# Attention values by head pairs in channel layout, and a merge written out unit by unit

## What is computed

```python
o_a = rms_norm(gated_delta_rule(...)) * silu(dn_z)          # branch 0
o_b = block_sweep_attention(b_qf, b_kf, b_v, scale, None)   # branch 1
o_c = rms_norm(gla_chunked(...)) * silu(gla_g)              # branch 2
o_d = block_sweep_attention(fox_q, fox_k, fox_v, scale, forget_cum)   # branch 3

# block_sweep_attention, for each block of 128 queries and each of 4 heads
logits = (q[block] @ k[:end].T) * scale (+ forget terms), masked
p = softmax(logits)
out = p @ v[:end]

merged = 0
for i in range(4):
    gate = sigmoid(h @ w_gate[i] + b_gate[i])
    merged = merged + gate * (branches[i] @ w_branch_up[i])
x = x + rms_norm(merged @ w_out, norm_mix_post)
```

## Time and profile before

| | |
|---|---|
| runs | 3096.55, 3099.35, 3099.67 us; median 3099.35 |
| profiled execution | 3094.74 us, span 3093.0 us |
| TensorE busy | 2818.3 us (91%), 14648 instructions |
| VectorE, ScalarE busy | 1431.7 us (46%), 952.0 us (31%) |
| mean granted TensorE clock | 0.966 |

### The profile page before, as it was taken

How to read it: one execution, slowest core, us unless ns; L and a number is a source line. 1 busy time by engine, 2 the same in 40 slices (tenths; PEclk the granted TensorE clock), 3 DMA queues, 4 the chain that set the end, 5 groups by cost and what they waited for, 6 DMA issues and landing times. The chain is left out here.

```text
span 3093.0 us, 35149 instructions
## 1 busy us (share of the span) xinstructions
PE 2818.3 (91%) x14648; PEld 2196.2 (71%) x14648; DVE 1431.7 (46%) x1621; ACT 952.0 (31%) x1291; POOL 121.2 (4%) x185
## 2 busy tenths in 40 slices
PE   6999998889978898987999999999389989999988
PEld 5767776567756676775888888888177768877776
DVE  2164442533142234846433434233746779842943
ACT  3141122333122433433323323121236622223122
POOL 0001110000000200100000100000000000000000
PEclk9999999999999999998999999999699999999999
DMA  3120011101112104621333333111320121112331
GB/s 105 43 74 32 29 39 56 55 29 48 52 47 72 49 23 159 212 63 48 109 96 96 102 96 98 53 48 48 122 75 28 48 68 58 52 41 96 106 116 68
DMA packets 66095, 220.81 MB, mean 71 GB/s; under 512 B 7608, under 2 KB 12504, under 8 KB 64288
## 3 DMA queue, kind: packets, MB, share of 16 engines
q1 hardware_dynamic: 51552, 165.01, 16.2%
q0 software_dynamic: 14400, 53.75, 5.1%
HBM read 179.93 MB, written 38.80 MB: 71 GB/s over the span
## 5 line engine op out<-in xcount | busy, mean ns | idle before, releaser
L280 PE MATMUL psum<-mixer_in,weights_parts 128*128 128x512 f32 x2112 | 504.4, 399 | 19.2 <-PEq L184 16.4
L280 PEld LDWEIGHTS psum<-mixer_in,weights_parts 128*128 128x128 f32 x2112 | 398.5, 189 | 118.4 <-issue 17.8
L424 PE MATMUL psum<-hidden,weights_parts 128*128 128x512 f32 x1536 | 433.8, 424 | 41.7 <-ACT early_gate L448 22.1
L247 DVE TENSOR_TENSOR weights_parts<-weights_raw,weights_parts 128x1024 fp32r<-128x1024 f32 (+2 forms) x195 | 211.4, 1084 | 386.7 <-ACT weights_parts L231 386.5
L424 PEld LDWEIGHTS psum<-hidden,weights_parts 128*128 128x128 f32 x1536 | 286.0, 195 | 127.4 <-issue 33.3
L280 PE MATMUL psum<-mlp_in,weights_parts 128*128 128x512 f32 x1536 | 352.3, 391 | 1.5 <-PEq L2418 1.5
L280 PE MATMUL psum<-mlp_hidden,weights_parts 128*128 128x512 f32 x1536 | 352.2, 391 | 0.0
L280 PEld LDWEIGHTS psum<-mlp_in,weights_parts 128*128 128x128 f32 x1536 | 288.4, 188 | 65.3 <-issue 2.3
L280 PEld LDWEIGHTS psum<-mlp_hidden,weights_parts 128*128 128x128 f32 x1536 | 288.5, 188 | 63.1
L280 PE MATMUL psum<-hidden,weights_parts 128*128 128x512 f32 x1200 | 279.2, 395 | 11.4 <-PEq L812 6.6
L231 ACT CAST weights_parts<-weights_raw 128x1024 fp32r<-128x1024 f32 (+2 forms) x195 | 182.2, 935 | 337.9 <-PE psum L280 223.7
(11 more groups left out here) (450 smaller groups left out, 3212.8 us busy)
## 6 DMA issues: line engine op xcount, KB each, us to landing
weights_raw<-in_w_in SPq DMA_DIRECT2D x73, 512.0 KB, 3.6
weights_raw<-in_w_mlp SPq DMA_DIRECT2D x64, 512.0 KB, 3.6
mod_weights<-in_mod_w POOLq DMA_DIRECT2D x80, 256.0 KB, 3.8
weights_raw<-in_w_gate SPq DMA_DIRECT2D x32, 512.0 KB, 3.7
gate_scratch<-early_gate SPq DMA_DIRECT2D x64, 256.0 KB, 2.2
gate<-gate_scratch POOLq DMA_DIRECT2D x32, 512.0 KB, 4.2
weights_raw<-in_w_out SPq DMA_DIRECT2D x24, 512.0 KB, 3.6
x_tokens<-in_x SPq DMA_DIRECT2D x4, 1024.0 KB, 8.1
```

The costliest lines, as they stand in the source:

```text
L247: nc.vector.tensor_tensor(c.parts[:, s, 1, 0:w], c.raw[:, s, 0:w], c.parts[:, s, 0, 0:w].bitcast(F32), ALU.subtract).then_inc(c.low_ready, 1)
L280: mm = nc.tensor.matmul(c.psum[:, bank + h, 0:cols], c.parts[:, s, wp, at], moving(k, xp, h), start=(n < halves), stop=(n >= halves * (3 * ...
L424: mm = nc.tensor.matmul(c.psum[:, bank, :], c.parts[:, s, wp, at], self.hidden[:, k, xp, h * HALF:(h + 1) * HALF], start=(k == 0 and n == ...
```

## The change

- `attend` multiplies the values of two heads at once, every second turn: v is the weights, the transposed probabilities move, and the heads of a pair write partitions 0 to 63 and 64 to 127. The output has channels on the partitions and is written to the branch's tile in SBUF. The reciprocal sums are spread over the channels by small products with the identity. The transposed probabilities have four buffers in place of two. The gate half is copied before the exponential of a turn.
- Branches 1 and 3 have no turning block; all 64 portions lie in `attend`, and halves from 4 on use bank 7. No branch is stored in DRAM. The turning of branches 0 and 2 writes to SBUF.
- The merge is written out as 32 units in the order `MERGE`, with units of branch 0 ahead; the branches are split tile by tile at units 0 to 2; a gate is loaded as soon as it is stored and its buffer is free; a bank is free after the product.
- The residual x is loaded by POOL in `mix_out`. Some scratch tiles of `latent_inputs`, `forgetting_inputs` and `add_residual` lie in others.

```diff
             @block.sync
             def _(sp):
-                if meanwhile:
-                    meanwhile(sp)
-                early.sp(sp, half)
-                if out is None:
-                    sp.wait_ge(vecs.sem, vecs.value("out"))
-                    store(c, sp, out_dram, o[:])
                 early.sp(sp, whole)
-                if out is None:
-                    sp.wait_ge(c.scratch_stored, c.stored)
         for s in (act, vecs, pes):
             s.end()
...
+def latent_attention(nc, c, t, hidden, small, early, out):
 
     with ExitStack() as ctx:
-        o_tok = c.sb("mla_out_tokens", [P, BLK, 256], ctx=ctx)
         v_tok = c.sb("mla_value_tokens", [P, BLK, 256], ctx=ctx)
         q, k = (c.sb(n, [P, HEADS, S], ctx=ctx) for n in ("mla_q", "mla_k"))
         with ExitStack() as inner:
             latent = c.sb("mla_latent", [P, 3, S], ctx=inner)
             project(nc, c, t["w_in"], 10, 3, hidden, latent)
-            early.begin(6, hidden, lambda half: 7 if 4 <= half < 10 else 6 + half % 2,
+            early.begin(6, hidden, lambda half: 7 if half >= 4 else 6 + half % 2,
                         (t["w_in"], 13, KT))
             latent_inputs(nc, c, t, latent, small, q, k, v_tok, early)
-        attend(nc, c, t, 0, 96, q, k, v_tok, o_tok, early, 48)
-        tokens_to_channels(nc, c, o_tok, t["branch"][1], early, 16)
+        attend(nc, c, t, 0, 96, q, k, v_tok, out, early, 64)
         early.end()
 
...
-                pe_spec.append(f"values{n - 1}")
+            if n and n % 2 == 0:
+                pe_spec += [(f"values{n // 2 - 1}", 2)]
                 if n % 4 == 0:
-                    vec_spec += [f"inverse{n // 4 - 1}", f"out{n // 4 - 1}"]
+                    pe_spec.append((f"spread{n // 4 - 1}", 2))
+                    vec_spec += [f"{s}{n // 4 - 1}" for s in ("inverse", "kept", "out")]
...
                     nk = (n // 4 + 1) * P
+                    early.act(a, upto(n - 1))
                     a.wait_ge(vecs.sem, vecs.value(f"max{n}"))
                     if n >= 2:
                         a.wait_ge(pes.sem, pes.value(f"turned{n - 2}"))
                     nc.scalar.activation(
                         prob[:, n % 2, 0:nk], scores(n, slice(0, nk)), ACT.Exp,
                         bias=neg_max[:, n % 2:n % 2 + 1], accum_out=sums[:, n:n + 1]).then_inc(act.step(f"exp{n}"), 1)
-                    early.act(a, upto(n - 1))
                     a.wait_ge(pes.sem, pes.value(f"turned{n}"))
-                    if n >= 2:
-                        a.wait_ge(pes.sem, pes.value(f"values{n - 2}"))
+                    if n >= 4:
+                        a.wait_ge(pes.sem, pes.value(f"values{n // 2 - 2}"))
                     m = min(nk, HALF)
-                    nc.scalar.copy(turned[:, n % 2, 0:m], c.psum[:, 4, 0:m]).then_inc(
+                    nc.scalar.copy(turned[:, n % 4, 0:m], c.psum[:, 4, 0:m]).then_inc(
                         act.step(f"low{n}"), 1)
                 early.act(a, e + portions)
...
                     v.wait_ge(act.sem, act.value(f"exp{4 * b + 3}"))
                     nc.vector.reciprocal(sums[:, s], sums[:, s]).then_inc(
                         vecs.step(f"inverse{b}"), 1)
-                    v.wait_ge(pes.sem, pes.value(f"values{4 * b + 3}"))
-                    v.wait_ge(vecs.sem, vecs.value(f"inverse{b}"))
+                    v.wait_ge(pes.sem, pes.value(f"spread{b}"))
+                    nc.vector.tensor_copy(spread[:], c.psum[:, 6, 256:512]).then_inc(
+                        vecs.step(f"kept{b}"), 1)
+                    v.wait_ge(vecs.sem, vecs.value(f"kept{b}"))
                     nc.vector.tensor_tensor(
-                        heads(o_tok[:, b, :]), heads(c.psum[:, 6, 0:256]),
-                        bcast(sums[:, s], DH), ALU.mult).then_inc(vecs.step(f"out{b}"), 1)
+                        out[:, :, b * P:(b + 1) * P],
+                        c.psum[:, 6, 0:256].rearrange("p (t n) -> p t n", t=2),
+                        spread[:].rearrange("p (t n) -> p t n", t=2), ALU.mult).then_inc(
+                        vecs.step(f"out{b}"), 1)
 
                 for n in turns:
...
+                def values(pair):
+
+                    b, t = pair // 2, pair % 2
+                    for m in (2 * pair, 2 * pair + 1):
+                        p.wait_ge(act.sem, act.value(f"low{m}"))
+                        if b >= 4:
+                            p.wait_ge(vecs.sem, vecs.value(f"high{m}"))
+                    if b and t == 0:
+                        p.wait_ge(vecs.sem, vecs.value(f"out{b - 1}"))
+                    for x in range(b + 1):
+                        for h in range(2):
+                            n = 2 * t + h
+                            last = mm(c.psum[64 * h:64 * h + 64, 6, t * P:(t + 1) * P],
+                                      v_tok[:, x, 64 * n:64 * n + 64],
+                                      turned[:, n, x * P:(x + 1) * P], start=(x == 0),
+                                      stop=(x == b))
+                            if x == b:
+                                last.then_inc(pes.step(f"values{pair}"), 1)
+
+                def spread_sums(b):
+
+                    p.wait_ge(vecs.sem, vecs.value(f"inverse{b}"))
+                    for t in range(2):
+                        for h in range(2):
+                            n = 4 * b + 2 * t + h
+                            last = mm(c.psum[64 * h:64 * h + 64, 6, 256 + t * P:256 + (t + 1) * P],
+                                      sums[:, n:n + 1].broadcast_to([P, DH]), c.ident[:],
+                                      start=True, stop=True)
+                            if t:
+                                last.then_inc(pes.step(f"spread{b}"), 1)
 
...
-                    if n:
-                        m = n - 1
-                        b, h = m // 4, m % 4
-                        p.wait_ge(act.sem, act.value(f"low{m}"))
-                        if b >= 4:
-                            p.wait_ge(vecs.sem, vecs.value(f"high{m}"))
-                        if b and h == 0:
-                            p.wait_ge(vecs.sem, vecs.value(f"out{b - 1}"))
-                        for x in range(b + 1):
-                            last = mm(c.psum[:, 6, 64 * h:64 * h + 64],
-                                      turned[:, m % 2, x * P:(x + 1) * P],
-                                      v_tok[:, x, 64 * h:64 * h + 64], start=(x == 0),
-                                      stop=(x == b))
-                        last.then_inc(pes.step(f"values{m}"), 1)
+                    if n and n % 2 == 0:
+                        values(n // 2 - 1)
+                        if n % 4 == 0:
+                            spread_sums(n // 4 - 1)
...
+MERGE = [(j, 0) for j in range(4)] + [
+    unit for j in range(8) for unit in [(j, 1), (j, 2), (j, 3)] + [(j + 4, 0)] * (j < 4)]
+SPLIT_AT = {0: [0, 1], 1: [2], 2: [3]}
...
+            for u in range(len(MERGE)):
+                for h in range(NH):
+                    pool.wait_ge(early.stored[h], 16 * (u + 1))
+                if u >= 4:
+                    pool.wait_ge(c.dve_done, d0 + sum(per_unit[:u - 3]))
+                pool.dma_start(gate[:, u % 4, :], t["gate"][u]).then_inc(loaded[u % 4], 16)
+
+        def sigmoid(a, u, j):
+            for x in SPLIT_AT.get(u, []):
+                for k in range(2):
+                    nc.scalar.copy(o[:, 2 * x + k, 0, :], plain[:, x, k]).then_inc(
                         act.step("high"), 1)
...
+            to, (j, q) = gate[:, u % 4, :], MERGE[u]
+            a.wait_ge(loaded[u % 4], 16 * (u // 4) + 16)
+            nc.scalar.activation(to, to, ACT.Sigmoid,
+                                 bias=vec(c, "b_gate", 4 * j + q)).then_inc(c.act_done, 1)
...
+        def low(v, u, j):
+            for x in SPLIT_AT.get(u, []):
+                for k in range(2):
+                    v.wait_ge(act.sem, act.value("high", 2 * x + k))
+                    nc.vector.tensor_tensor(o[:, 2 * x + k, 1, :], plain[:, x, k],
+                                            o[:, 2 * x + k, 0, :].bitcast(F32),
...
+            pe.wait_ge(vecs.sem, vecs.value("low", 2 * MERGE[u][1] + k))
...
+        def add(dve, u, s, result, act_count, dve_count, n, _):
+            j, q = MERGE[u]
             dve.wait_ge(c.act_done, act_count(u))
-            out = merged[:, bass.ds(j, 1), :].rearrange("p a n -> p (a n)")
-            to = gate[:, q, :] if q else out
-
-            nc.vector.tensor_tensor(to, gate[:, q, :], result,
-                                    ALU.mult).then_inc(c.dve_done, 1 if q else 2)
+            if not q:
+                dve.wait_ge(vecs.sem, vecs.value("low", j))
+            to = gate[:, u % 4, :] if q else merged[:, j, :]
+            nc.vector.tensor_tensor(to, gate[:, u % 4, :], result,
+                                    ALU.mult).then_inc(c.dve_done, 1)
             if q:
                 dve.wait_ge(c.dve_done, dve_count(u))
```

(16 more changed lines are left out.)

237 lines of the change are left out of this document (93 added, 144 removed).

## The result

The changed kernel takes **3048.54 us** (median of 4 runs, 3044.68 to 3051.76) where the kernel before takes 3097.97 on the same chip: a ratio of 0.984, 95% interval 0.9823 to 0.9857, or 49 us less. The forecast was 27 to 28 us less, with a range that ended at 3060. The direction and each place of the gain were right; the size was not. The profiled execution took 3044.68 us (span 3042.9), the fastest of its four; before, 3094.74 (3093.0).

A forecast was written before the change was run, and what follows sets the result against it. TensorE was taken as the engine to follow, losing time in waits and at stage ends. Attentions 14.6, first attention's end 4.2, third branch 3.4 and merge start 5.5 sum to 27.7 us less: 3072 us, range 3060 to 3092.

The forecast's parts named there:

- values and spread, with the transposes beside them, both attentions: Attentions: paired value passes overlap in two column halves, 0.056 us apart; less spread and visits, 6.5 us gained per attention.
- turns that waited for a gate's copy, both: Attentions: TensorE's waits for the copy of a gate half go, 3.8 us gained per attention.
- turns without values, both: Attentions, blocks 4 to 7: turns without value passes no longer cover the chain to the next exponential, 2.8 us lost per attention.
- turns behind a finished block, both: Attentions: finishing a block adds 0.46 us to the chain against 0.31 more gate work, seven times: 1.0 us lost per attention.
- end of the first attention: Between first attention and next projection: no turning stage, 5.0 us saved less a charge for the lower clock, 4.2 us.
- end of the third branch: Third branch's block end: no wait for its store and no lower clock behind it, 3.4 us saved.
- start of the merge, to unit 4: Merge start: no turning stage, branches split tile by tile, unit 4 starting 18.0 us in; 5.5 us saved.
- rest of the merge: Merge from unit 4 on: period stays 6.2 us per two units, the relaxed bank wait does not act; 0 gained.
- the softmax chain: Attentions: path from transposes to next exponential; turns without values lose 2.8 us, block finishes 1.0, per attention.
- rival 2: The softmax chain holds both attentions, gaining 0 to 1 us each instead of 7.3: 3085 us; chance 0.16.
- rival 3: Starts cost less: no lower clock at the merge or after the attention, visits half as dear: 3064 us; chance 0.14.
- Rival 4: Branch loads and store were already hidden and VectorE sets the merge's start: without 5.5 and 3.4, 3081 us; chance 0.10.

The follow-up runs named there:

- pairs with 48 portions: Changed kernel with 48 gate portions in each attention and the other 16 in a block of their own behind it: 3074.71 us, ratio 0.9942.
- the copy first alone: Kernel before with only the gate half's copy moved ahead of the exponential (48 portions, no pairs): 3087.55 us, ratio 0.997.
- the kernels with 64 portions and the copy behind: Copy behind the exponential, 64 portions per attention: kernel before so altered, without pairs, 3134.03 us; changed kernel so altered, with pairs, 3090.29 us.
- the kernel with 64 portions and no pairs: Kernel before with the gate copy ahead of the exponential, 64 portions per attention and none in the stage behind: 3091.57 us, ratio 0.9988.

## Why the prediction was too small

Terms of the sum, us saved, forecast and measured (profiled executions, 50.1 between their spans). For the attentions the starts of TensorE's passes give each turn's time; half of its time at the lower clock is taken off, and so are its score passes, 0.448 us for 512 keys, and its gate passes, 0.229. Turn 17, which is both, counts with the turns that waited for a copy. What is left, before less after, is summed over the turns of a kind:

| step | forecast | measured |
|---|---|---|
| values and spread, with the transposes beside them, both attentions | 13.0 | 14.6 |
| turns that waited for a gate's copy, both | 7.6 | 7.9 |
| turns without values, both | -5.6 | -2.4 |
| turns behind a finished block, both | -2.0 | +5.5 |
| last head, both | 1.6 | 1.7 |
| other turns, both | 0 | 0.2 |
| lower clock, both | 0 | 3.2 |
| attentions, sum (0.1 unplaced) | 14.6 | 30.8 |
| end of the first attention | 4.2 | 5.6 |
| end of the third branch | 3.4 | 3.9 |
| start of the merge, to unit 4 | 5.5 | 7.8 |
| rest of the merge | 0 | 2.9 |

(Attentions: 130.1 + 11.0 - 124.1 = 17.0 and 127.8 + 11.0 - 125.0 = 13.8. End of the first: 770.74 - 752.84 - 11.0 against 750.77 - 749.50. Merge: 25.4 against 1193.24 - 1175.63 = 17.6. What remains of the 50.1, about -1, is a third branch 2.5 us longer, in which a wait for weights took 3.1 instead of 1.3, a first attention that starts 2.7 later, and 4.2 gained behind the merge. The first is a cost of the change that the forecast did not have: to its last transposes that branch takes 189.1 to 190.7 us in the eight traces with the new code and 187.7 to 189.9 in the six with the old; which edit does it was not traced. The other two are scatter as far as can be seen: behind the merge the fourteen traces take 1759.5 to 1767.7 us, the first attention starts at 621.8 to 625.8, and the changed kernel's own executions differ by 7 us.)

**The step that failed is the softmax chain, "Per attention 6.5 + 3.8 - 2.8 - 1.0 + 0.8", and in it the -1.0.** It gave the turns that finish a block "0.31 more gate work", about what the 16 portions come to when they are spread evenly over the turns (11.0 / 33 = 0.33). The schedule in the code is not even. In whole portions, turns 5 and 9 go from 1 to 3, turn 13 from 2 to 3, turns 25 and 29 from 1 to 2: just the turns behind a finished block, where TensorE of the kernel before waited 0.66, 0.68, 1.15, 0.78 and 0.82 us for its exponential. Two portions are 1.38. These waits are the larger part of the 6.3 us of idle time that stands in the earlier trace rows, and the sum let them stand, and added to them. Turn 13 of the first attention, kernel before, then changed, then pairs with 48 portions:

```profile
658.54 1.96 PE L424 MATMUL psum<-hidden,weights_parts 128*128 128x512 f32 x6
661.59 0.66 PE L2190 MATMUL psum<-identity,attention_probs 128*128 128x128 f32 x4 [1.09 <-ACT attention_probs L2110]
```

```profile
661.71 2.66 PE L425 MATMUL psum<-hidden,weights_parts 128*128 128x512 f32 x9
664.21 0.60 PE L2198 MATMUL psum<-identity,attention_probs 128*128 128x128 f32 x4
```

```profile
663.29 0.66 PE L2221 MATMUL psum<-identity,attention_probs 128*128 128x128 f32 x4 [1.44 <-ACT attention_probs L2108]
```

After the change turns 5, 9 and 13 wait for nothing and turns 17, 21, 25 and 29 for some 0.4 each: +2.8 us per attention where -1.0 was forecast. The turns without values (-5.6) were priced at twice what they cost (-2.4): by starts TensorE loses next to nothing by them in block 4 and 0.2 to 0.5 us at turns 22, 24, 26, 28 and 30. Without the extra portions the pairs gain nothing at all: with 48 portions the attention is 0.6 and 0.4 us *longer* with pairs than with the copy first alone, with 64 portions 4.6 and 5.3 shorter than without pairs (all with the clock out). So rival 2, the chain that holds both attentions, described a true mechanism; with 64 portions it was bought off. The forecast treated the moved portions as a cost carried from one stage into another, when they were the filler that made the pairs pay. Of the 22 us that the sum of 27.7 lacks, 7.5 are in the turns behind a finished block, 3.2 in those without values, 3.2 in the clock and 5.2 in the merge.

**The copy waits** came out at 7.9 for 7.6, and at 7.7 with the copy first alone; the agreement is partly luck. The idle column has 3.8 us, but from start to start the five turns with such a wait are 5.1 us longer than their passes. The ends of TensorE's matmuls are computed and not observed, says the Trainium skill, Perfetto Trace Analysis, section Tensor Engine Instruction; that the idle column comes out smaller than the time from start to start, the rows here bear out. Of the 5.1 us, 1.1 stay when the copy is ahead: at turn 11 TensorE then waits for the exponential instead (0.34 idle); what holds the rest, most of it at turn 6, was not traced. What the copy ahead avoids is larger than what it removes: 15 to 23 us per attention (12 to 15 with the clock out), which the kernels with 64 portions and the copy behind lose. This could have been read: the forecast itself placed the halves' ends at heads 4, 8, 12.

**Values.** The passes were right at 0.055 us against 0.056. The rule on row groups of the Trainium skill (TensorE: Matmul & The Clock Gate, Part 3), by which the kernel would have been slower, is not borne out in any run here: passes that use all rows, each with its own weights, are 0.055 us apart. The visits were dearer in the forecast, 5.1, than they are, some 3.9: value and spread passes take 21.7 us and lengthen the transposes by 1.6, of which 352 x 0.055 = 19.4 is work.

**Stage ends** were right in kind: TensorE restarts after 1.28 and 1.41 us, where 1.9 and 1.5 were forecast, and no lower clock follows the first attention, for which 0.8 was charged. **The merge's start** came at 17.6 instead of 19.9; ScalarE's copies and VectorE's subtractions took what was forecast, the first unit started after 2.5 us instead of 3.0. **The merge's loop:** "From unit 4 on I expect nothing" was right about the relaxed wait and missed the loop written out, 0.26 us per two units over the 14 such pairs of units.

None of the four rivals gives the measured time. Of rival 3 only the clock behind the first attention came true (the 0.8 above). Rival 4 does not hold: the branch loads and the store were not wholly hidden, as the kernel with 64 portions and no pairs shows (9.7 of 11.0, and 1.8 more).

## What to carry to other kernels

Work that moves into a stage is not a cost to be carried across at its own length: read in which turns it lands, against the waits that TensorE has in just those turns, and count whole portions by the schedule in the code, not their mean. Where a result has to leave a bank on an engine that also runs the critical chain, put its copy ahead of the instruction that waits, and look at whether it falls due where the chain is longest. In a loop bound by a chain over one engine, only what stands between the release and the next need counts: moving a 1.2 us sum behind a 0.4 us cut gave 5.7 us. And before lengths are compared between traces, take out what ran at the lower clock: 5.5 and 4.0 us became 3.8 and 3.9.

## What the runs showed of the hardware

- Fp32 passes of 128 columns with 64-column weights are 0.109 us apart in one half of the columns and 0.055 on average when they alternate between the halves (0.007 within a pair, 0.110 from pair to pair), with all 128 rows in use by both. Without alternation about four passes still run beside four of the other half where the one ends and the other begins.
- In the merge's loop TensorE's first matmul follows the start of its cut by 0.67 us, in the same code written out by 0.47.
- An attention spends between 3.4 and 27.5 us at the lower clock. The two kernels in which TensorE waits over 2 us at seven turns have most of it, up to 26.1 and 27.5 us in the second attention; the others have at most 13.9. What sets it at the start of an attention was not tried.
